# A chunked scan of two recurrences: no products with a zero state in the first chunk, no state work in the last, and three small table copies moved

## What is computed

```
# _ssd, one chunk: c, b, xdt are projections, acs the running sum of log decays
y_off  = einsum(c, state) * exp(acs)              # zero where state is zero
y      = y_diag + y_off + xs * d_skip             # y_diag: inside the chunk
new_state = state * exp(acs[-1]) + einsum(b, exp(acs[-1] - acs), xdt)
y      = rms_per_group(y * silu(z)) * norm_g

# _mlstm, one chunk
num    = einsum(s, v) + w_inter * einsum(q, c_mem)   # second term zero at first
den    = sum(s) + w_inter * einsum(q, n_mem)
h      = num / max(|den|, exp(-m))
c_new  = dec * c_mem + einsum(g, k, v)            # nobody reads the last one
```

## Time and profile before

| | |
|---|---|
| median of 3 runs | 1574.43 us (1573.89 to 1575.0) |
| the profiled execution | 1573.38 us, of which the traced span is 1571.6 us |
| busy share of the span | PE 97%, PEld 84%, DVE 58%, ACT 41%, POOL 36% |
| granted TensorE clock, mean | 0.992 of full |
| the scan block | from 559.96 to 761.50 us, one ordinary chunk about 22.1 us |

### The profile page before, as it was taken

The page is one execution under the profiler, slowest core; times in us unless marked ns, Lnnn a source line. Parts: engine busy times, 40 slices in busy tenths (PEclk is TensorE's granted clock), DMA queues, the critical chain, the costliest instruction groups (busy, mean ns, idle before and its releaser), DMA issues.

```text
span 1571.6 us, 23657 instructions
## 1 busy us (share of the span) xinstructions
PE 1525.6 (97%) x9114; PEld 1314.0 (84%) x9114; DVE 907.6 (58%) x1484; ACT 649.0 (41%) x1272; POOL 566.1 (36%) x325
## 2 busy tenths in 40 slices
PE   8999999999999999999999999999999999999897
PEld 7798989898999987877788877888888888787686
DVE  7675878684843469999344272345544245554623
ACT  6542534353532233444345252345555333556321
POOL 3245454545344346567565330132212013211110
PEclk9999999999999999999999999999999999999899
DMA  5133333333334345765675330122111112113612
GB/s 178 41 122 94 122 94 121 94 121 94 121 108 135 100 160 186 227 199 175 220 267 201 121 94 14 28 61 76 53 54 34 34 28 80 54 35 114 254 67 107
DMA packets 151085, 176.43 MB, mean 112 GB/s; under 512 B 9671, under 2 KB 126659, under 8 KB 149955
## 3 DMA queue, kind: packets, MB, share of 16 engines
q1 hardware_dynamic: 150810, 174.92, 34.2%
q10 hardware_dynamic: 168, 0.06, 0.0%
HBM read 122.46 MB, written 52.43 MB: 111 GB/s over the span
## 4 chain that ended last, share of the span: by engine, by line
PE 47%; DVE 1%; ACT 1%; issue 1%; DMA 1%; POOL 0%; SPq 0%; POOLq 0%; ACTq 0%; DVEq 0%
PE b_ps L2404 22%; PE b_ps L2449 4%; PE b_ps L2424 4%; PE b_ps L2354 3%; PE b_ps L2356 3%; PE b_ps L2355 3%; PE b_ps L2436 2%; PE b_ps L2506 2%; PE b_ps L2507 2%; PE b_ps L2508 2%; PE b_ps L2457 1%; PE b_ps L2372 0%; DMA b_yy<-z 0%; DMA z<-b_y_T 0%; ACT a_aT L2056 0%
## 5 line engine op out<-in xcount | busy, mean ns | idle before, releaser
L1925 POOL TENSOR_TENSOR b_w<-b_w_raw,b_w 128x1024 fp32r<-128x1024 f32 x66 | 158.4, 2400 | 357.5 <-DVE b_w L2184 253.6
L2404 PE MATMUL b_ps<-a_h_hi,b_w 128*128 128x512 f32 x768 | 265.7, 406 | 2.9 <-DVE a_h_lo L2162 2.9
L393 POOL TENSOR_TENSOR b_w<-b_y_T,b_w 128x1024 fp32r<-128x1024 f32 x54 | 141.1, 2615 | 189.7 <-ACT b_w L451 189.7
L2404 PEld LDWEIGHTS b_ps<-a_h_hi,b_w 128*128 128x128 f32 x768 | 145.0, 189 | 37.1 <-issue 3.9
L2404 PE MATMUL b_ps<-a_h_lo,b_w 128*128 128x512 f32 x384 | 150.6, 392 | 0.0
L941 PE MATMUL b_ps<-b_w,p_hi 128*128 128x256 f32 x768 | 139.2, 283 | 0.0
L700 DVE SCALAR_TENSOR_TENSOR b_w_raw<-p_out_raw,p_cols,b_w_raw 128x1024 f32<-128x1024 f32 x60 | 119.8, 2003 | 12.8 <-ACT b_w_raw L482 11.4
L941 PEld LDWEIGHTS b_ps<-b_w,p_hi 128*128 128x128 f32 x768 | 120.1, 192 | 0.6
L941 PE MATMUL b_ps<-b_w,p_lo 128*128 128x256 f32 x384 | 108.7, 283 | 0.0
L2195 DVE CUSTOM_DVE_ANT_0 b_y_T<-b_ps,a_neg_dist 128x128 f32<-128x128 f32 (+5 forms) x96 | 72.1, 777 | 63.3 <-PE b_ps L2424 52.7
L451 ACT CAST b_w<-b_y_T 128x1024 fp32r<-128x1024 f32 x60 | 62.7, 1045 | 106.5 <-DVE b_y_T L661 55.0
(11 more groups left out here) (417 smaller groups left out, 3616.6 us busy)
## 6 DMA issues: line engine op xcount, KB each, us to landing
b_y_T<-in_ab_w_in SPq DMA_DIRECT2D x33, 512.0 KB, 4.3
tok<-p_out_raw SPq DMA_DIRECT2D x64, 256.0 KB, 2.3
b_w_raw<-in_ab_w_out SPq DMA_DIRECT2D x32, 512.0 KB, 3.7
b_w_raw<-in_c_w_in SPq DMA_DIRECT2D x32, 512.0 KB, 4.1
feat<-b_w_raw SPq DMA_DIRECT2D x20, 512.0 KB, 2.7
c_fe<-feat SPq DMA_DIRECT2D x7, 1280.0 KB, 6.6
yt<-b_y_T SPq DMA_DIRECT2D x8, 1024.0 KB, 10.9
b_y_raw<-yt SPq DMA_DIRECT2D x32, 256.0 KB, 3.9
```

Of the source, the lines that this page charges most:

```text
L393: gp.tensor_tensor(w_lo[s % SLOTS][:, :, :], operand(n, split_of(n, p))[:, :, :], w_hi[s % SLOTS][:, :, :].bitcast(F32), ALU.subtract).the ...
L1925: gp.tensor_tensor(w_lo[:, w, :], w_raw[u % W_RAW][:, :], w_hi[:, w, :].bitcast(F32), ALU.subtract).then_inc(S["l_wlo"], 1)
L2404: mm = pe.matmul(o, x, y, start=(k == 0 and q == 0), stop=(k == KT - 1 and q == 2))
```

## The change

All of it is in `scan_chunks`:

- In chunk 0 TensorE no longer multiplies by `cmem` (L1277) and by `state` (L1287); VectorE has no t1 (L1597) there and copies ydiag instead of adding (L1603). GpSimd's decay of the state in chunk 0 no longer waits for yoff.
- In chunk 7 TensorE does not turn the keys (L1050), and makes no new memory and state (L1302, L1308); VectorE leaves out c_dec, e_end, gk, kg, the memory and state updates; GpSimd leaves out xe and the decay of the state. What followed waits for other semaphores (`d_h`, and `d_t1`).
- VectorE's `low_y(0)` and `low_y(1)` of chunk 7 stood behind the first y and behind the state update; now both stand at the end of `weights` of chunk 7, ahead of the second turn of chunk 6.
- GpSimd's third `low_unit` of chunk 7 stood behind the gate product; now it stands ahead of y plus skip.
- In chunks 0 to 6 the three table copies stood between the memory and the state update; now they stand ahead of the memory update.
- TensorE's first decay rows of a chunk waited for all four memory updates; now for the first and the second of them.

```diff
@@ TensorE @@
-                    pe.wait_ge(S["d_cmem"], n * 4)
+                    pe.wait_ge(S["d_cmem"], n * 4 - 3)
                     decays(n, par, 0)
+                    pe.wait_ge(S["d_cmem"], n * 4 - 2)
                     decays(n, par, 1)
...
                 for h in range(ML_HEADS):
-                    pe.matmul(ps[:, 4 + h, 0:VW], st[:, h, :], va[par][:, h, :], start=True, stop=False)
-                    mm = pe.matmul(ps[:, 4 + h, 0:VW], qs[:, h, :], cmem[:, h, :], start=False, stop=True)
+                    mm = pe.matmul(ps[:, 4 + h, 0:VW], st[:, h, :], va[par][:, h, :], start=True, stop=not behind_first(n))
+                    if behind_first(n):
+                        mm = pe.matmul(ps[:, 4 + h, 0:VW], qs[:, h, :], cmem[:, h, :], start=False, stop=True)
                     mm.then_inc(S["p_num"], 1)
...
-                for k in range(2):
+                for k in range(2) if behind_first(n) else ():
                     mm = pe.matmul(ps[:, 2 + k, :], f[:, CT + k, :], state[:, k * 512:(k + 1) * 512], start=True, stop=True)
...
+                if is_last(n):
+                    return
                 for h in range(ML_HEADS):
                     pe.wait_ge(S["d_h"], n * 4 + (h + 1))
                     mm = pe.matmul(ps[:, 4 + h, 0:VW], kg[:, h, :], va[par][:, h, :], start=True, stop=True)
...
-            pe.wait_ge(S["d_cmem"], 4 * TILES)
+            pe.wait_ge(S["d_h"], 4 * TILES)
             for u in (0, 1):
                 mid_products(u, (2, 3, 1))
@@ GpSimd @@
+                if not is_last(n):
...
                 spare(0)
                 spare(1)
+                spare(2)
                 gp.wait_ge(S["d_y"], n * 2 + 2)
...
-                spare(2)
                 gp.wait_ge(S["d_meany"], n + 1)
@@ VectorE @@
                 turned()
                 ssd_weights(1)
+                if is_last(n):
+                    low_y(0)
+                    low_y(1)
+                    return
...
+                if not is_last(n):
+                    next_tables()
+                    dve.wait_ge(S["p_cmem"], n + 1)
+                    for h in range(ML_HEADS):
+                        dve.scalar_tensor_tensor(out=cmem[:, h, :], in0=cmem[:, h, :], scalar=c_dec[:, h:h + 1],
+                                                 in1=ps[:, 4 + h, 0:VW], op0=ALU.mult, op1=ALU.add).then_inc(S["d_cmem"], 1)
```

More of the change, by code:

```diff
@@ L1108, in scan_chunks @@
         behind_first = lambda n: not isinstance(n, int) or n > 0
+        is_last = lambda n: isinstance(n, int) and n == TILES - 1
         feats = lambda n, par: fe[par][:, 0:KTL, :] if behind_first(n) else chunk["first_fe"]
@@ L1242, in weights @@
                 decays(n, par, 3)
-                if behind_first(n):
+                if behind_first(n) and not is_last(n):
                     turn_keys(pe, ps, kt, ident, S)
@@ L1537, in weights @@
                 dve.wait_ge(S["d_cmem"], n * 4)
[L1538 removed]
+                if not is_last(n):
+                    dve.tensor_copy(c_dec[:, :], b4(7)[:, :, P - 1:P].rearrange("p h a -> p (h a)")).then_inc(S["d_cdec"], 1)
                 dve.wait_ge(S["a_wm"], n + 1)
@@ L1592, in outputs @@
                                              op1=ALU.mult).then_inc(S["d_h"], 1)
-                for k in (0, 1):
+                for k in (0, 1) if behind_first(n) else ():
                     c = slice(k * 512, (k + 1) * 512)
-                    dve.wait_ge(S["p_yoff"], n * 2 + (k + 1))
+                    dve.wait_ge(S["p_yoff"], n * 2 + (k - 1))
                     dve.tensor_tensor(hd(t1[:, c]), hd(ps[:, 2 + k, :]),
```

67 lines of the change are left out of this document (33 added, 34 removed).

## The result

The changed kernel took 1580.02 us (median of 6 runs, 1576.04 to 1581.34), the kernel before beside it 1574.72: ratio **1.0029**, 95% interval 1.0016 to 1.0042. It is slower by 0.3%, and outside the predicted range. The profiled execution has a span of 1578.4 us against 1571.6.

| stretch | before | after | difference |
|---|---|---|---|
| start of the scan to the first product of the heads, chunk 0 | to 569.07 | to 570.33 | +1.26 |
| chunk 0, heads to heads | 20.99 | 18.11 | -2.88 |
| chunks 1 to 6 | 132.13 | 132.18 | +0.05 |
| heads of chunk 7 to layer2's first product | 40.71 | 46.78 | +6.07 |
| from there to the end | 808.7 | 811.0 | +2.3 |

The account below looks back on a forecast made before the run. TensorE, busy 97% of the span, was taken as the bound: the end moves only where it pauses or has work to leave out. Terms -2.3 + 0 + 2.2 + 0.4 = +0.3 us gave a median of 1574.7, range 1570.6 to 1578.6.

Parts of the forecast that it names:

- Chunk 0: First chunk: zero products dropped, ydiag then waits for kg, chunk 1 starts earlier; -2.3 us, bounds -2.43 to -0.7.
- Chunks 0 to 6: Tables and waits: tables held by GpSimd's skip, delay hidden by GpSimd's chain; 0 per chunk, six chunks -0.6 to +1.5.
- Rival 1: VectorE's tables, chunks 0 to 6, held through GpSimd's power too; six chunks 3.6 us slower, 1578.3; chance 0.10.
- Chunk 7, order: Last chunk: low_y held, ydiag later, GpSimd's unit 2 ahead of the skip awaiting its cast, TensorE pausing 5.2 us for h.
- Chunk 7, size: Last chunk: unit 2's data 5.0 us after asking, skip 4.1 late; costs +2.2 us, bounds -1.6 to +3.5.
- The clock: Low clock stretch around TensorE's long pause before turning h in chunk 7; +0.4 us, bounds 0 to +2.75.
- rival 3: Chunk 7: clock stays low for two stretches behind the long pause, 2.75 instead of 0.4; 1577.0; chance 0.13.
- The sum: Whole kernel: chunk 0, chunks 0 to 6, chunk 7 and clock together give +0.3 us, median 1574.7.
- Rival 2: Chunk 7: both low_y get through together, unit 2 asked for at 728.5, skip only 1.3 late; 1571.0; chance 0.19.

Follow-up runs that it names:

- b1: Kernel before with only the tables in front of the memory update and TensorE's two relaxed waits behind it; ratio 0.9996.
- a3: Changed kernel with both chunk 7 orders put back: third weight unit behind the gate product, low_y behind the first y and ahead of h's gates; ratio 0.9976.
- a4: Kernel before with only the products, sums and waits of chunk 0 as changed; ratio 1.0000.
- b4: Changed kernel with SyncE issuing unit 2's loads ahead of the store of chunk 6's first half of y; ratio 0.9984.
- c1: Changed kernel with both TensorE pauses of chunk 7 filled by transposes, 15 ahead of yoff and 48 before the turning of h; ratio 1.0002.
- b3: Changed kernel with 24 transposes filling TensorE's pause before the turning of h in chunk 7; ratio 1.0031.
- d4: Changed kernel with 15 transposes ahead of yoff, filling only TensorE's pause before ydiag in chunk 7; ratio 1.0029.
- c2: b4 with low_y(0) behind the turned pieces, low_y(1) behind y, and ScalarE's cast of unit 2's weights ahead of h's squares; ratio 0.9964, 1570.16 us.
- d2: c2 with ScalarE's cast of unit 2's weights back behind the squares of h; ratio 1.0010.
- d3: Changed kernel plus twelve products meant for TensorE's two scan-start pauses; only the second pause went, chunk 0 computes other values; ratio 1.0003.
- d1: c2 plus the same scan-start products as d3, chunk 0 again computing other values; ratio 0.9954.
- e1: c2 with 6 products in the second of TensorE's scan-start pauses alone, in a free bank; ratio 0.9974.

## Why the prediction was wrong, point by point

- **Chunk 0.** Forecast -2.3, measured -2.88 in this chunk, and 3.3 from the scan's start to chunk 1 between two profiles with equally much low clock (b1 and a3). The mechanism is as told (ydiag waits for kg, the decay of the state is out of the way), but kg came earlier than taken, and the mean was not held; in a4 it was (576.27, 1.45 us). The sum treated chunk 0 and the tables as independent, and they are not: a4 shows that without the tables in front the gain is eaten by a wait of 3.94 us.
- **Chunks 0 to 6.** Forecast 0, measured +0.05 for six chunks, and b1 confirms it. Rival 1 (held through the power) is refuted: the two small tables ran in 0.21 and 0.16 beside it. The rule of the Trainium skill ("SBUF — State Buffer", section "Who interferes with whom") that the prediction weighed fits the large table beside the skip (2.38 us) and not the small ones beside the power.
- **Chunk 7, order.** Right in kind: `low_y` twice held (1.74 and 2.83 us singly, 4.49 together), a pause in front of ydiag, the third unit ahead of the skip and waiting for its cast, TensorE waiting for h (3.90 us; forecast 5.2). a3 shows that the whole loss hangs on the two orders.
- **Chunk 7, size: this step failed.** "With the 1 MB store beside it I take 5.0": the y of unit 2 was there 7.5 us behind the moment when SyncE began to ask for unit 2 (736.46 against 728.93). SyncE itself stood 1.81 and 1.23 us in issuing the two loads behind the store, and the DMA share was 0.99; which of the two sets the landing stays open. The moment of asking was right (8.31 behind the heads). The skip came 19.85 - 13.38 = 6.5 late relative to the heads instead of 4.1, h 3.8 late instead of 1.6. b4 shows by itself that the place behind the store is what counts: with the loads ahead of it the loss turns into a gain. In the forecast's own terms the last chunk with the clock was to cost 2.6, and cost 6.07: 2.2 more up to h, from this term, and the rest behind h, mostly the clock.
- **The clock: too small as well.** I took +0.4, bounds up to +2.75. The profiles of the changed kernel against c1's show 1.3 to 1.9 at layer2. That is rival 3's case in part: the first profile has 6.83 us at 0.50 over the turning of h and what follows, two stretches of 3.41 as that rival had it, at 1.9 instead of 2.75. The pause in front of ydiag got no price, though the forecast had it; in L2 it cost nothing, as its low stretch was hidden. In the medians c1 is 4.2 us under the changed kernel, while b3 and d4 are not under it at all; where that comes from is not shown.
- **The sum.** -2.9 + 0.05 + 6.1 is 3.2 of the profiled 6.8; the start of the scan (+1.26) and the part behind layer2 (+2.3) lie outside what was forecast. The tail took 811.0 and 810.5 in the two profiles of the changed kernel, 808.7 before, 807.5 in b4 and 807.7 in c2, but 811.1 in d2, 812.0 in d3 and 810.5 in a4; these five long ones show three low stretches of 3.41 us behind 1440 us. But d1 (811.4) and e1 (810.3) are as long with two stretches (10.24 and 3.41, 6.83 and 3.41), and the short ones have one or two, so the number of stretches alone does not tell a long tail from a short one. What picks the one or the other stays open, and so does why d4 and b3, whose profiled executions took 1576.8 and 1575.8, have medians of 1580.5 and 1581.1.
- **Rival 2** (unit 2 in time, 1571.0). In the changed kernel its condition was not met: `low_y(1)` was held, and the loads were asked for 8.31 behind the heads, as in the forecast, not 6.3. b4 comes near its time (0.9984 of 1574.7 is 1572.2) by asking ahead of the store, but with the skip still 3.6 late instead of 1.3. c2 has the skip no later than before (13.00 against 13.38 behind the heads) and 0.9964.

## What to carry to other kernels

Work that is taken off the last stage shows only if what fills the idle engines has its data: when a filler is moved ahead of the chain's next step on an in-order engine, follow its data back to the DMA's issue and to the queue it stands in, and try to issue those loads ahead of any large store. Price each new pause of TensorE at both levels of the clock, and look whether another wait hides the stretch. Two edits that each measure as nothing (a4, b1) can be worth about 3 us together (estimated from b1 and a3), so test the pair before dropping either.
